# Entry of the second feed-forward block: statistics and normalising of tiles 4 to 7 placed behind the first half's modulation

## The chip, the core and the metric

The kernel runs on one core of a Trainium2 chip. Five engines work from queues of their own and meet only at semaphores: TensorE (PE, matrix products and transposes), VectorE (DVE), ScalarE (ACT), GpSimd (POOL) and SyncE (SP, which starts transfers). The metric is the device time of the whole program in microseconds (us), taken as the median of several runs. The rows shown here come from one profiled execution.

## What is computed

One layer of an encoder on 1024 positions of 1024 values, in fp32: a feed-forward block, a token mixer, and a second feed-forward block. The change touches only how the second feed-forward block begins.

```python
def _layer_norm(x):
    xf = x.astype(jnp.float32)
    mu = jnp.mean(xf, axis=-1, keepdims=True)
    var = jnp.mean(jnp.square(xf - mu), axis=-1, keepdims=True)
    return (xf - mu) * lax.rsqrt(var + LN_EPS)

def _swiglu(u, w_gate, w_up, w_down):
    return (jax.nn.silu(u @ w_gate) * (u @ w_up)) @ w_down

# in reference(), for each of the three sublayers
u = (_layer_norm(h) * (1.0 + scale) + shift).astype(h.dtype)
z = DEEPNORM_ALPHA * h.astype(jnp.float32) + resid_w * gate * fn(u)
return (_layer_norm(z) * ln_g[layer, j] + ln_b[layer, j]).astype(h.dtype)
...
h = sublayer(h, 2, lambda u: _swiglu(u, ffn2_w_gate[layer], ffn2_w_up[layer], ffn2_w_down[layer]), 0.5)
```

## The kernel before

The program is a row of phases with a barrier between them: the first feed-forward block (tag f1), the boundary into the mixer, two attention phases, the output projection, and the second feed-forward block (tag f2). Both blocks are `ffn_phase`. The rows give the tiles of both with one name (`f_...`); everything shown here lies in f2. The activations h are 8 tiles of 128 positions in `acc`; the tiles 0 to 3 are the first half (512 positions) and 4 to 7 the second.

**From h to the operands of the products.** For each tile VectorE takes the statistics (`ln.statistics`, lines 267 to 269: two bn_stats and an aggregate); ScalarE takes the root (`ln.root`, L278); VectorE works out the coefficients of a pair of tiles (`ln.coefficients`, L288 to L292); ScalarE writes the normalised tile (`ln.normalise`, called through `enter`, L297) into `f_nrm`. TensorE turns 128x128 blocks of it (`turn(y)`, L1272: four transposes, one 128x512 block in one of four PSUM banks). `turn(0)` to `turn(7)` are the first half, `turn(8)` to `turn(15)` the second; the first waits for 4 normalised tiles, the eighth for all 8. A turned block is modulated (scaled and shifted): the even y on VectorE (L1069), the odd ones on ScalarE (L887).

**fp32 in three products.** Each factor is split into a rounded high part, copied by ScalarE, and the low rest, subtracted by VectorE. `high0` and `low0` (L894, L1075) split the first half's blocks, `hi(o)` and `lo(o)` (L906, L1080) the weights of operand o, the lines 992, 994, 1153 and 1156 the second half's blocks. One product is 12 matmuls (4 steps of depth by high*high, high*low, low*high).

**The products at the entry.** `plain_product(p)`, p from 0 to 15, are the plain ones: p 0 to 7 work on the first half and p 8 to 15 on the second. Product p waits for its weights, `w_lo >= p % 8 + 1`. p 0 to 3 need the operands 0 to 3, p 4 to 7 the operands 4 to 7. The operands 0 to 3 are split among the first half's modulations. The operands 4 to 7 are split in the loop over k that treats the second half: in step k ScalarE and VectorE first modulate and split the second half's block k, and then operand 4 + k. The products after the plain ones (`product(j, i)`) also need sums of blocks that GpSimd takes from the modulated blocks (L843, L847, L850, L855).

**What sets the order.** It is written out by hand: each engine runs the instructions in the order of the code, and waits in front of one that isn't ready hold back all behind it. TensorE issues turns 0 to 7, products 0 and 1, turns 8 to 11, product 2, turns 12 to 15, product 3 and the rest. VectorE takes all 8 statistics, with the coefficients of tiles 0 to 3 among them, then the first half's modulation and splitting, and then the coefficients of tiles 4 to 7. ScalarE takes the roots of all tiles before the first half's copies, and normalises tiles 4 to 7 behind them. In f1 the tiles come normalised (`ready` is true, `ln` is None).

Of the kernel before, what the change touches and what calls it, by code (L numbers as in the profile page):

```python
# [18 lines left out]
KT = D // P  # L19
TT = S // P  # L20
# [607 lines left out]
def ffn_phase(nc, top, tag, mem, weights, j_mod, gate, resid, acc, mod_col, ident, hid, h_in, ada, lng, lnb, out,  # L628
# [67 lines left out]
    with ExitStack() as st:  # L696
        ps = Parts(nc, st).ps(tag + "_ps", [P, 8, NB])
        ln = None if ready else Normaliser(nc, top, mem.small, tag + "_in")
# [10 lines left out]
        def source(o):  # L709
            if o < RING:  # L710
                _, kk, j, f = plain(o)
                return raw[:, j, HK * kk:HK * kk + HK, P * f:P * f + P]
            j, i = seq[o - RING]
            r = raw[:, j % 2]
            if i == 1:
                return r[:, 0:HK, 0:P]
            if i == 2:
                return r[:, HK:KT, 0:P]
            if i == 4:
                return r[:, HK:KT, P:2 * P]  # L720
            return sums[:, (5, 6, 3, 7).index(i)]
# [7 lines left out]
        def half1(y):  # L729
            return (y - KT) // 2 + HK * (y % 2)  # L730
# [149 lines left out]
        def _(act):  # L880
# [88 lines left out]
            def enter(t):  # L969
                ln.normalise(act, nrm[t // 4][:, t % 4, :], acc[:, t, :], t)  # L970

            if ln is not None:
                for g in range(TT // 4):
                    ln.root(act, g)
                    enter(2 * g)
                    enter(2 * g + 1)
                for g in range(TT // 4, TT // 2):
                    ln.root(act, g)
            for y in range(HK):
                high0(y)  # L980
            for y in range(HK, KT):
                hi(y - HK)
                high0(y)
            if ln is not None:
                for t in range(TT // 2, TT):
                    enter(t)
            if keep is not None:
                act.wait_ge(kept, 16 * TT)
            for k in range(HK):
# [72 lines left out]
        def _(dve):  # L1062
# [62 lines left out]
            if ln is not None:  # L1125
                for t in range(TT // 2):
                    ln.statistics(dve, acc[:, t, :], t)
                    if t % 2:
                        ln.coefficients(dve, t // 2)
                for t in range(TT // 2, TT):  # L1130
                    ln.statistics(dve, acc[:, t, :], t)
            for y in range(KT):
                if y % 2 == 0:
                    modulate(y)
# [5 lines left out]
            lo(HK - 1)  # L1140
            low0(KT - 1)
            if ln is not None:
                ln.coefficients(dve, 2)
                ln.coefficients(dve, 3)
            if keep is not None:
                dve.wait_ge(kept, 16 * TT)
                dve.wait_ge(ln.normed, TT)
# [116 lines left out]
        def _(pe):  # L1264
            def turn(y):
                if ln is not None:
                    pe.wait_ge(ln.normed, TT // 2 * (y // KT + 1))
                if y >= 4:
                    pe.wait_ge(mod_done[y % 2], (y - 4) // 2 + 1)
                k = y if y < KT else half1(y)  # L1270
                for g in range(TT // 2):
                    done = nc.tensor.transpose(ps[:, TURN[y % 4], P * g:P * g + P],  # L1272
                                               nrm[y // KT][:, g, P * k:P * k + P], ident[:, :])
                done.then_inc(tr_done, 1)
# [10 lines left out]
            def plain_product(p):  # L1285

                half, kk, j, f = plain(p)
                o = p % 8
                pe.wait_ge(w_lo, o + 1)
                if half == 0:  # L1290
                    pe.wait_ge(lo0, HK * (kk + 1))
                    high, low = ((B11, B11), (B21, B21))[kk]
                else:
                    pe.wait_ge(mod_done[0], KT)
                    pe.wait_ge(mod_done[1], KT)
                    pe.wait_ge(lo_b if kk else lo_a, HK)
                    high, low = ((T4, T2), (B22, B22))[kk]
                multiply(PLAIN_BANK[half][j][f], o, uh[:, high], ul[:, low], kk == 0, kk == 1)
# [31 lines left out]
            def modulate(h):  # L1330
# [10 lines left out]
                                            start=h % 2 == 0, stop=h % 2 == 1, skip_group_check=True)  # L1341
                done.then_inc(a_mm, 1)

            for y in range(KT):
                turn(y)
            for p in range(PLAIN):
                plain_product(p)
                if p in (1, 2):
                    for y in range(4):
                        turn(KT + 4 * (p - 1) + y)  # L1350
            h = 0
            for n in range(PLAIN, N):
                product(*seq[n - PLAIN])
# [718 lines left out]
```

## Time and profile before

| | us |
|---|---|
| median of 3 runs | 2240.72 |
| lowest, highest | 2240.2, 2241.95 |
| span of the profiled execution | 2239.6 |

| engine | busy us, share of the span |
|---|---|
| TensorE, matmuls and transposes | 2040.5 (91%) |
| VectorE | 1100.8 (49%) |
| ScalarE | 753.1 (34%) |
| GpSimd | 462.5 (21%) |

In the profile L12 is line 12 of the kernel, and x4 is four instructions told in one row. A name of the form `f_ul<-acc,f_uh` is the tile written and the tiles read. "PEclk" is the clock that TensorE was granted, as a share of its full 2.4 GHz; only 1.00 and 0.50 (1.2 GHz) occur, and a number between them is a stretch that has some of each. The ends of matmuls are modelled, so starts are the better guide.

### The profile page before, as it was taken

What the parts mean: (1) busy time and instruction counts of PE and PEld (TensorE: products, weight loads), DVE (VectorE), ACT (ScalarE), POOL (GpSimd) and SP (SyncE); (2) the same over time, 40 slices, a digit from 0 to 9 for tenths busy, and PEclk for the clock granted to TensorE, in tenths of its full rate; (3) what the DMA queues carried; (4) which work ended last, traced back from release to release, by engine and by line L of the source; (5) the groups of instructions that cost most, each with busy time, mean ns of one, the idle gap of its engine ahead of it and who ended that gap; (6) DMA issues with size and microseconds to landing.
All of it is one profiled execution on the core that took longest, in us unless ns stands there. A gap on an engine that the chain in (4) does not pass through costs nothing. (4 is left out here: it accounts for less than half of the span.)

```text
span 2239.6 us, 27243 instructions
## 1 busy us (share of the span) xinstructions
PE 2040.5 (91%) x10350; PEld 1585.9 (71%) x10350; DVE 1100.8 (49%) x1891; ACT 753.1 (34%) x1253; POOL 462.5 (21%) x332
## 2 busy tenths in 40 slices
PE   3999999999999938999988889794999999999997
PEld 2777777777888826766666666673888888878885
DVE  4854544454346473344324443467743444443556
ACT  2533323333223243244323433315433333332331
POOL 0622222220004120000033202231622222100041
PEclk6999999999999969999999999897999999999998
DMA  6253444444644021100133021503222222265341
GB/s 254 82 160 124 157 156 130 155 142 168 246 147 167 30 104 47 57 28 29 56 82 60 19 49 38 197 38 120 76 89 74 90 80 90 90 237 195 141 168 49
DMA packets 157608, 247.34 MB, mean 110 GB/s; under 512 B 8097, under 2 KB 106673, under 8 KB 157361
## 3 DMA queue, kind: packets, MB, share of 16 engines
q1 hardware_dynamic: 126370, 211.36, 27.3%
q10 hardware_dynamic: 30096, 30.25, 4.4%
q0 software_dynamic: 1024, 4.13, 1.2%
q8 instruction: 77, 1.26, 0.2%
q14 instruction: 41, 0.34, 0.0%
HBM read 205.09 MB, written 40.63 MB: 110 GB/s over the span
## 5 line engine op out<-in xcount | busy, mean ns | idle before, releaser
L1280 PE MATMUL f_ps<-f_uh,f_ops 128*128 128x512 f32 x2496 | 794.1, 395 | 9.0 <-DVE acc L1119 4.9
L1280 PEld LDWEIGHTS f_ps<-f_uh,f_ops 128*128 128x128 f32 x2496 | 470.5, 188 | 137.8 <-issue 28.0
L1280 PE MATMUL f_ps<-f_ul,f_ops 128*128 128x512 f32 x1248 | 491.1, 394 | 0.0
L1380 PE MATMUL f_ps<-f_wdh,f_hdh 128*128 128x512 f32 x704 | 273.9, 389 | 0.0
L1380 PE MATMUL f_ps<-f_wdl,f_hdh 128*128 128x512 f32 x704 | 273.9, 389 | 0.0
L1380 PE MATMUL f_ps<-f_wdh,f_hdl 128*128 128x512 f32 x704 | 273.9, 389 | 0.0
L1280 PEld LDWEIGHTS f_ps<-f_ul,f_ops 128*128 128x128 f32 x1248 | 235.4, 189 | 48.2
L1180 DVE TENSOR_TENSOR f_wdl<-f_wd,f_wdh 128x2048 fp32r<-128x2048 f32 x44 | 107.3, 2438 | 227.2 <-ACT f_wdh L1010 227.2
L868 POOL TENSOR_TENSOR f_sums<-f_raw 128x512 f32<-128x512 f32 x80 | 107.4, 1343 | 444.4 <-DVE f_ops L1080 359.8
L1080 DVE TENSOR_TENSOR f_ops<-f_sums,f_ops 128x512 fp32r<-128x512 f32 x160 | 118.6, 741 | 153.9 <-ACT f_ops L906 153.9
L1010 ACT CAST f_wdh<-f_wd 128x2048 fp32r<-128x2048 f32 x44 | 83.9, 1907 | 302.5 <-PE f_ps L1380 259.5
L1754 PE MATMUL in_pj<-ut_hi,in_wh 128*128 128x512 f32 x376 | 151.1, 402 | 9.2 <-PEq L2036 4.8
L1080 DVE TENSOR_TENSOR f_ops<-f_raw,f_ops 128x512 fp32r<-128x512 f32 x136 | 99.0, 730 | 114.2 <-ACT f_ops L906 114.1
L1380 PEld LDWEIGHTS f_ps<-f_wdh,f_hdh 128*128 128x128 f32 x704 | 132.3, 188 | 27.7
L1380 PEld LDWEIGHTS f_ps<-f_wdl,f_hdh 128*128 128x128 f32 x704 | 132.2, 188 | 27.5
L1380 PEld LDWEIGHTS f_ps<-f_wdh,f_hdl 128*128 128x128 f32 x704 | 132.1, 188 | 27.3
L1754 PE MATMUL in_pj<-ut_lo,in_wh 128*128 128x512 f32 x376 | 148.2, 394 | 0.0
L1754 PE MATMUL in_pj<-ut_hi,in_wl 128*128 128x512 f32 x376 | 148.2, 394 | 0.0
L1119 DVE TENSOR_TENSOR acc<-acc,f_ps 128x512 f32<-128x512 f32 x120 | 82.5, 688 | 132.5 <-PE f_ps L1280 132.3
L875 POOL TENSOR_TENSOR acc<-acc,f_rows 128x1024 f32<-128x1024 f32 x12 | 36.1, 3006 | 384.5 <-ACT acc L297 384.5
L906 ACT CAST f_ops<-f_sums 128x512 fp32r<-128x512 f32 x160 | 95.6, 618 | 37.4 <-PE f_ps L1280 16.7
L906 ACT CAST f_ops<-f_raw 128x512 fp32r<-128x512 f32 x136 | 81.0, 620 | 31.8 <-PE f_ps L1280 21.0
(212 smaller groups left out, 2652.2 us busy)
## 6 DMA issues: line engine op xcount, KB each, us to landing
f_wd<-in_ffn_w_down SPq DMA_DIRECT2D x44, 1024.0 KB, 4.9
f_raw<-in_ffn_w_gate SPq DMA_DIRECT2D x22, 1024.0 KB, 5.5
f_raw<-in_ffn_w_up SPq DMA_DIRECT2D x22, 1024.0 KB, 5.4
f_hidden<-acc SPq DMA_DIRECT2D x88, 256.0 KB, 2.2
f_hd<-f_hidden SPq DMA_DIRECT2D x44, 512.0 KB, 5.6
f_aw<-in_w_ada ACTq DMA_DIRECT2D x28, 512.0 KB, 3.6
acc<-in_w_ada ACTq DMA_DIRECT2D x28, 512.0 KB, 3.5
in_raw<-in_w_in SPq DMA_DIRECT2D x24, 512.0 KB, 6.7
```

The costliest lines, as they stand in the source:

```text
L868: nc.gpsimd.tensor_tensor(sums[:, x], of, with_, how).then_inc(s_done, 1)
L875: nc.gpsimd.tensor_tensor(acc[:, t, :], acc[:, t, :], mem.rows[:, 0, :], ALU.mult).then_inc(gained, 1)
L906: nc.scalar.copy(op(o)[0], source(o)).then_inc(w_hi, 1)
L1010: nc.scalar.copy(mem.wdh[n % 3][:, :, :], mem.wd[:, n % 2]).then_inc(wd_hi, 1)
L1080: nc.vector.tensor_tensor(op(o)[1], source(o), op(o)[0].bitcast(F32), ALU.subtract).then_inc(w_lo, 1)
L1119: nc.vector.tensor_tensor(to, t_in, ps[:, bank, :], ALU.add).then_inc(done, 1)
L1180: nc.vector.tensor_tensor(mem.wdl[n % 3][:, :, :], mem.wd[:, n % 2], mem.wdh[n % 3][:, :, :].bitcast(F32), ALU.subtract).then_inc(wd_lo, 1)
L1280: done = nc.tensor.matmul(ps[:, bank, :], l[:, k, :], r[:, k, :], start=fresh and k == 0 and m == 0, stop=closed and k == HK - 1 and m == ...
L1380: done = nc.tensor.matmul(ps[:, b, :], l[n % 3][:, c, P * t:P * t + P], r[n % 3][:, c, NB * (b % 2):NB * (b % 2) + NB], start=p == 0 and c ...
L1754: last = nc.tensor.matmul(pj[:, half, :], l[:, k, j, :], r[:, k, NB * half:NB * half + NB], start=(k == 0 and n == 0), stop=(k == KT - 1 a ...
```

## The change

It moves instructions on three engines and adds or takes away none. On VectorE the statistics of tiles 4 to 7 go from ahead of the first half's modulation to behind it, in pairs with their coefficients. On ScalarE the roots of the tiles 4 to 7 go behind the first half's copies, each pair's roots ahead of its normalising. On TensorE, in f2 alone, turns 8 to 11 follow product 3 (they followed product 1) and turns 12 to 15 follow product 4 (they followed product 2). The transfers and GpSimd's instructions stay as they are.

```diff
@@ scalar engine
                     ln.root(act, g)
                     enter(2 * g)
                     enter(2 * g + 1)
-                for g in range(TT // 4, TT // 2):
-                    ln.root(act, g)
             for y in range(HK):
                 high0(y)
             for y in range(HK, KT):
                 hi(y - HK)
                 high0(y)
             if ln is not None:
-                for t in range(TT // 2, TT):
-                    enter(t)
+                for g in range(TT // 4, TT // 2):
+                    ln.root(act, g)
+                    enter(2 * g)
+                    enter(2 * g + 1)
@@ vector engine
                     if t % 2:
                         ln.coefficients(dve, t // 2)
-                for t in range(TT // 2, TT):
-                    ln.statistics(dve, acc[:, t, :], t)
             for y in range(KT):
...
             low0(KT - 1)
             if ln is not None:
-                ln.coefficients(dve, 2)
-                ln.coefficients(dve, 3)
+                for t in range(TT // 2, TT):
+                    ln.statistics(dve, acc[:, t, :], t)
+                    if t % 2:
+                        ln.coefficients(dve, t // 2)
@@ tensor engine
+            TURN_AFTER = (1, 2) if ready else (3, 4)
             for y in range(KT):
                 turn(y)
             for p in range(PLAIN):
                 plain_product(p)
-                if p in (1, 2):
+                if p in TURN_AFTER:
                     for y in range(4):
-                        turn(KT + 4 * (p - 1) + y)
+                        turn(KT + 4 * TURN_AFTER.index(p) + y)
```

On VectorE, where the first half's modulation begins and where the first half's splitting ends, before (`f_in_sm` holds the statistics, `f_b1m` the first half's modulated blocks, `f_ops_12698` the operands 0 to 3, `f_ops_12703` the operands 4 to 7):

```order
L268 BN_STATS f_in_sm<-acc 128x6
L269 BN_AGGR f_in_sm<-f_in_sm 128x2
L1069 TENSOR_SCALAR f_b1m<-f_ps,mod_col 128x512 x2
...
L1075 TENSOR_TENSOR f_ul<-f_b1m,f_uh 128x512
L288 RECIPROCAL f_in_sm<-f_in_sm 128x2
...
L292 SCALAR_TENSOR_TENSOR f_in_sm<-f_in_sm 128x2
L1069 TENSOR_SCALAR acc<-f_ps,mod_col 128x512 x2
L1153 TENSOR_TENSOR f_ul<-acc,f_uh 128x512
L1156 TENSOR_TENSOR f_ul<-acc,f_uh 128x512
L1080 TENSOR_TENSOR f_ops_12703<-f_raw,f_ops_12703 128x512
```

The same two places on VectorE in the changed kernel:

```order
L292 SCALAR_TENSOR_TENSOR f_in_sm<-f_in_sm 128x2
L1069 TENSOR_SCALAR f_b1m<-f_ps,mod_col 128x512 x2
...
L1075 TENSOR_TENSOR f_ul<-f_b1m,f_uh 128x512
L267 BN_STATS f_in_sm<-acc 128x6
L268 BN_STATS f_in_sm<-acc 128x6
L269 BN_AGGR f_in_sm<-f_in_sm 128x2
...
L292 SCALAR_TENSOR_TENSOR f_in_sm<-f_in_sm 128x2
L1069 TENSOR_SCALAR acc<-f_ps,mod_col 128x512 x2
L1153 TENSOR_TENSOR f_ul<-acc,f_uh 128x512
L1156 TENSOR_TENSOR f_ul<-acc,f_uh 128x512
L1080 TENSOR_TENSOR f_ops_12703<-f_raw,f_ops_12703 128x512
```

The modulation of the first half now follows the coefficients of tiles 2 and 3 directly, and the splitting of the first half is followed by four tiles' statistics and two sets of coefficients where only the two sets of coefficients stood.

On TensorE, around turns 8 to 15, before (`f_nrm_12705` holds the normalised tiles 4 to 7):

```order
L1280 MATMUL f_ps<-f_uh,f_ops_12698 128x512
L1272 MATMUL f_ps<-ident,f_nrm_12705 128x128 x16
L1280 MATMUL f_ps<-f_uh,f_ops_12698 128x512
...
L1280 MATMUL f_ps<-f_uh,f_ops_12698 128x512
L1272 MATMUL f_ps<-ident,f_nrm_12705 128x128 x16
L1280 MATMUL f_ps<-f_uh,f_ops_12698 128x512
```

And in the changed kernel:

```order
L1280 MATMUL f_ps<-f_uh,f_ops_12698 128x512
L1272 MATMUL f_ps<-ident,f_nrm_12705 128x128 x16
L1280 MATMUL f_ps<-f_uh,f_ops_12703 128x512
L1280 MATMUL f_ps<-f_ul,f_ops_12703 128x512
...
L1280 MATMUL f_ps<-f_uh,f_ops_12703 128x512
L1272 MATMUL f_ps<-ident,f_nrm_12705 128x128 x16
L1280 MATMUL f_ps<-f_uh,f_ops_12703 128x512
```

Both sets of turns stood in front of products that read the operands 0 to 3; both now stand in front of products that read the operands 4 to 7.

## Rows read from the trace of the kernel before

**Rows 1.** Chain of work that ended last: start us, us, what.

```profile
1548.44 4.64 ACT f_nrm L297 x4
1553.13 3.67 PE f_ps L1272 x16
1556.80 3.09 PE f_ps L1280 x12
1559.89 1.75 PE f_ps L1272 x16
1561.64 410.02 PE f_ps L1280 x1800
```

**Rows 2.** TensorE's waits from 1561 us to the end: us in total, times, longest.

```profile
PE f_ps L1280 <- DVE acc L1119: 2.5, 1, 2.5
```

**Rows 3.** Timeline of VectorE, entry of f2: start, us, instruction [idle before <- releaser].

```profile
1522.13 0.69 DVE L267 BATCH_NORM_STATS2 f_in_sm<-acc 128x6 f32<-128x512 f32 x1 [0.91 <-PEq L2044]
...
1530.82 0.69 DVE L267 BATCH_NORM_STATS2 f_in_sm<-acc 128x6 f32<-128x512 f32 x1
...
1536.44 1.48 DVE L1069 TENSOR_SCALAR f_b1m<-f_ps,mod_col 128x512 f32<-128x512 f32 x2
...
1547.46 0.16 DVE L288 RECIPROCAL f_in_sm<-f_in_sm 128x2 f32<-128x2 f32 x1
```

**Rows 4.** Timeline of ScalarE, same stretch.

```profile
1530.94 2.37 ACT L297 ACTIVATE f_nrm<-acc,f_in_sm 128x1024 f32<-128x1024 f32 x2 [1.03 <-DVE f_in_sm L292]
```

**Rows 5.** Timeline of TensorE, same stretch.

```profile
1533.37 3.67 PE L1272 MATMUL f_ps<-ident,f_nrm 128*128 128x128 f32 x16 [24.93 <-ACT f_nrm L297]
...
1542.48 0.50 PE L1280 MATMUL f_ps<-f_uh,f_ops 128*128 128x512 f32 x1 [1.33 <-DVE f_ops L1080]
...
1553.13 3.67 PE L1272 MATMUL f_ps<-ident,f_nrm 128*128 128x128 f32 x16 [4.87 <-ACT f_nrm L297]
```

**Rows 6.** Timeline of VectorE, second half's steps k = 0 to 3.

```profile
1554.39 0.81 DVE L1069 TENSOR_SCALAR acc<-f_ps,mod_col 128x512 f32<-128x512 f32 x1 [5.11 <-PE f_ps L1272]
...
1556.72 1.71 DVE L1153 TENSOR_TENSOR f_ul<-acc,f_uh 128x512 fp32r<-128x512 f32 x1
...
1558.95 0.68 DVE L1080 TENSOR_TENSOR f_ops<-f_raw,f_ops 128x512 fp32r<-128x512 f32 x1
1560.37 0.81 DVE L1069 TENSOR_SCALAR acc<-f_ps,mod_col 128x512 f32<-128x512 f32 x1 [0.74 <-PE f_ps L1272]
...
1564.20 0.68 DVE L1080 TENSOR_TENSOR f_ops<-f_raw,f_ops 128x512 fp32r<-128x512 f32 x1
...
1567.71 0.68 DVE L1153 TENSOR_TENSOR f_ul<-acc,f_uh 128x512 fp32r<-128x512 f32 x1
...
1569.51 2.48 DVE L1084 TENSOR_TENSOR f_ul<-acc,f_uh 128x512 fp32r<-128x512 f32 x4
```

**Rows 7.** Timeline of TensorE: turns 12 to 15 and product 3.

```profile
1559.73 1.91 PE L1272 MATMUL f_ps<-ident,f_nrm 128*128 128x128 f32 x16
1561.39 0.48 PE L1280 MATMUL f_ps<-f_uh,f_ops 128*128 128x512 f32 x1
```

**Rows 8.** By stretch: us, busy of PE, PEld, DVE, ACT, POOL, then PEclk, DMA share, GB/s.

```profile
1533.00:1537.00 4.00, 3.63 (x16) 3.28 (x16) 3.90 (x9) 1.23 (x5) 0.00 (x0) 0.51 1.02 416
1537.00:1540.00 3.00, 1.73 (x13) 1.28 (x12) 2.36 (x5) 2.77 (x6) 0.00 (x0) 1.00 0.94 384
...
1550.00:1553.00 3.00, 0.00 (x0) 0.00 (x0) 0.00 (x0) 3.00 (x3) 0.00 (x0) 0.59 0.00 0
...
1980.50:1984.00 3.50, 3.50 (x11) 2.72 (x10) 0.00 (x0) 0.00 (x0) 0.00 (x0) 0.52 0.23 80
```

**Rows 9.** Timeline of TensorE around its one late wait.

```profile
1979.60 0.47 PE L1280 MATMUL f_ps<-f_uh,f_ops 128*128 128x512 f32 x1 [2.46 <-DVE acc L1119]
...
1980.99 1.06 PE L1280 MATMUL f_ps<-f_uh,f_ops 128*128 128x512 f32 x2
...
1982.27 1.06 PE L1280 MATMUL f_ps<-f_uh,f_ops 128*128 128x512 f32 x2
```

## The prediction

> **What bounds the kernel now.** I read the page first (TensorE busy 91% of the span), then the chain of work that ended last, and then the timelines of each engine through the entry of the second block. The chain says where time at the entry counts [rows 1]. Up to 1553.13 it runs through ScalarE, which normalises tiles 4 to 7 (4.64 us). From 1553.13 it runs through TensorE: 16 transposes (turns 8 to 11), 12 matmuls (product 2), 16 transposes (turns 12 to 15), and then 1800 matmuls in 410.02 us with nothing between them. From 1561 us to the end TensorE waits for another engine once, for 2.5 us [rows 2]. So TensorE is the bound from turn 8 on, and whatever reaches it later than now there is paid in full at the end; no slack follows that could give it back. I therefore compare the time at which product 8 (the first on the second half) can start. Now, product 3 starts behind the last turns at about 1561.6 and five products (3 to 7) follow. A product is 12 matmuls at 410.02 / 1800 = 0.228 us, that is 2.73 us, so product 8 starts at 1561.64 + 5 x 2.73 = **1575.3**.
>
> **Step 1, the first half starts earlier.** Turn 0 begins at 1533.37, as soon as tiles 0 to 3 are normalised (1530.94 + 2.37) [rows 4, 5], but VectorE modulates the first block only at 1536.44, behind the statistics of tiles 4 to 7, which began at 1530.82 [rows 3]. With these moved away it begins when the turn is ready. In the second half, turn 8 begins at 1553.13 and VectorE's modulation at 1554.39, 1.26 later [rows 5, 6]; so here 1533.37 + 1.26 = 1534.63, which is 1.81 us earlier. ScalarE's copies and modulations wait for VectorE's first one and pace the rest, so the whole first half moves by 1.8: product 0 from 1542.48 [rows 5] to 1540.7, the end of splitting on VectorE from 1547.46 [rows 3] to 1545.65. ScalarE's four roots, which move too, are hidden in the same way.
>
> **Step 2, the second half's normalising is late.** Behind 1545.65 VectorE now has four statistics and two sets of coefficients, between them roots and normalising on ScalarE: the very sequence that tiles 0 to 3 went through from 1522.13 [rows 3] to the start of turn 0 at 1533.37 [rows 5], 11.24 us. Turn 8 thus starts at 1545.65 + 11.24 = **1556.9**, against 1553.13 now: 3.8 us later. Ahead of it lie four products and not two: 1540.7 + 4 x 2.73 = 1551.6. TensorE waits 5.3 us, about what it waits now (4.87, [rows 5]). That alone would not be a loss, since two products (5.46 us) have been done in those 3.8 us: 1.7 us would be won.
>
> **Step 3, what stands behind the turns.** Now product 2 follows turn 11, and its weights are long split. In the changed kernel product 4 follows, and operand 4 is split by VectorE only behind the second half's modulations. Now it is ready at 1558.95 + 0.68 = 1559.63, 6.50 us behind the start of turn 8 [rows 5, 6]. Nothing in these 6.5 us depends on what TensorE runs behind the turns, so product 4 starts at 1556.9 + 6.5 = **1563.4**. The turns take 3.67 us at the low clock, as now [rows 5], to 1560.6; 2.8 us of new waiting. This is the wait that takes the old one's place.
>
> **Step 4, the clock.** TensorE's granted clock fell to 0.50 between 1550 and 1553, with TensorE idle since 1548.3 [rows 5], and was still low when the turns ran (3.67 us for 16, against 1.75 for turns 12 to 15) [rows 1, 8]. A wait of 5.3 us should do the same. Then come 3.67 us of transposes, 2.8 us of nothing and product 4. That a wait of this size is enough by itself shows late in the program: one of 2.46 us was followed by a stretch at 0.52 [rows 8, 9]; three matmuls start 1982.27 - 1980.99 = 1.28 us apart there, 0.427 each. So I take product 4 at 1.2 GHz: 12 x 0.427 = 5.1 us, to 1568.5. At 2.4 GHz it would take 2.73, to 1566.1; these are the two ends. I take the slow one, since the clock is low ahead of the turns and a wait lies on either side of them.
>
> Before turn 0, TensorE had run nothing for 24.93 us, and 16 transposes alone brought the clock from 0.51 to 1.00 [rows 5, 8]. The Trainium skill ("TensorE: Matmul & The Clock Gate", "Part 4: PE-mode transpose") says that the high clock doesn't engage for transposes, because they don't count as TensorE being busy; by that product 4 would be slow without exception, and the sum would be the one I take. The trace disagrees with that rule.
>
> **Step 5, the second set of turns.** Turns 12 to 15 now stand behind product 4, and VectorE's step k = 1 begins with the modulation of turn 12's block, ahead of operand 5. Now that modulation starts 0.64 us behind turn 12 at 2.4 GHz (1559.73 to 1560.37, [rows 6, 7]), or 1.26 at 1.2 GHz (step 1). Operand 5 is ready at 1564.20 + 0.68, 4.51 behind the modulation [rows 6], but two subtractions of this stretch are slow, running beside GpSimd; free of it, three take 1.8 together (1567.71 to 1569.51), and with the modulation's 0.8 that is 2.6 us. GpSimd has had its work for k = 1 in the meantime, so I take the short one, with the low clock: 1.26 + 2.6 = 3.9 us, between 3.2 (0.64 + 2.6) and 5.1 (0.64 + 4.51). Product 5 starts at 1568.5 + 3.9 = **1572.4**. TensorE's turns take 1.7 to 3.7 of it, so up to 2.2 us are waiting.
>
> **Step 6, products 5 to 7.** Operand 6 takes VectorE one such step more, 2.6 to some 3.4 with GpSimd beside it, say 3.0 us, against 2.73 for a product: 0.3 us. Operand 7 has no modulation on VectorE and is in time. Product 8 starts at 1572.4 + 3 x 2.73 + 0.3 = **1580.9**.
>
> **The sum.** 1580.9 - 1575.3 = 5.6 us later. By parts: the earlier first half -1.8, the later statistics +5.6 (together +3.8 at turn 8: 11.24 from the end of splitting to turn 8, where 5.67 pass now), two products already done -5.5, the wait for operand 4 +2.8, the clock +2.4, the second set of turns with the wait for operand 5 +2.2 over the 1.7 they cost now, and 0.3 for operand 6; product 2 at the low clock, which now costs 3.09 [rows 1] and not 2.73, is gone, -0.4. That is 5.5, and 5.6 before rounding. Nothing later is in danger of adding: the sums on GpSimd and the block splits move by the same 4 to 6 us and the products that need them move too. The second half's tile loads, stores and the copy of h to memory are not moved. The span would be 2239.6 + 5.6 = 2245.2; the median of the runs is 1.1 above the profiled span, so the forecast is 2240.7 + 5.6 = **2246.3**.
>
> **The rivals.** *A, forecast*: as above, +4.5 to +6.7. *B, the clock comes back*: the transposes of turns 8 to 11 raise it, as the first 16 did, and the wait behind them doesn't take it away. Product 4 saves 2.4 and turn 12 some 0.6: +2.6, up to +4.4 where the clock is high for a part; 2243.3. For it: the rise after transposes alone [rows 8]. Against: 2.46 us of waiting were enough for a fall [rows 9]. *C, all is hidden*: the other side. It takes the statistics, roots and normalising to be covered by products 0 to 3 and operand 4 to be split when the turns end. Then product 8 would start at 1540.7 + 8 x 2.73 + 2 x 1.75 = 1566.0, that is 9.3 us sooner: 2231.4. It decides at 5.9 us from the end of splitting (1545.65) to turn 8 (1551.6), where the same sequence now takes 11.24, and operand 4 has to be split within 1.75 us and not 6.5. If only operand 4 were in time, 1.7 us would be won: 2239.0. Against both stand rows 3 and 6, which are measured durations of these very instructions. *D, a second fall*: the waits before products 5 and 6 let the clock fall once more; such a stretch, 3.5 us at half clock [rows 8], costs 1.7, and slow subtractions beside GpSimd 1.2: +6.7 to +8.5, 2248.0.
>
> **How the numbers follow.** A 0.58, D 0.15, B 0.22, C with its half 0.03, and 0.02 for what I don't see, on either side. For this kernel 0.2% is 4.5 us, about what a measurement can tell from no change, and A's low end lies on it: a twelfth of A goes to "same". Slower: 0.53 + 0.15 + 0.01 = 0.69; same: 0.05 + 0.22 + 0.01 = 0.28; faster 0.03. The range goes from B, with 0.3 us for the medians, to the middle of D with 1 us more: 2243.0 to 2249.0. It leaves out C, the edges of B and D and the unseen, some 0.13.
>
> **What would show it.** In the changed kernel's timeline: VectorE's first L1069 some 1.8 us earlier behind turn 0; four products in a row, then a TensorE wait of about 5.3 us on ScalarE's L297; 16 transposes; a second wait of 2 to 3 us on VectorE's L1080; product 4 at the low clock, starts 0.427 apart; a wait on L1080 behind turns 12 to 15; and no wait of TensorE afterwards but the known one at the end of the gate and up products. Step 2 is wrong if turn 8 starts earlier than 1555, step 3 if no wait follows turn 11, step 4 if product 4 takes under 3 us. The forecast falls if TensorE starts product 8 before 1578.

## The result

| | us |
|---|---|
| changed kernel, median of 9 runs | 2245.16 (2242.47 to 2247.57) |
| kernel before, median of 9 runs | 2240.2 (2237.35 to 2241.95) |
| ratio | 1.0022, 95% interval 1.0013 to 1.0032 |
| span of the profiled execution | 2243.1 |

The change made the kernel slower by 5.0 us, 0.22%. The forecast was 5.6 us slower, 2246.3.

The first half's entry in the changed kernel. These are the timelines of TensorE and VectorE (start us, us, instruction, idle time before it and what ended it); they answer to [rows 5] and [rows 3]:

```profile
1532.61 4.84 PE L1272 MATMUL f_ps<-ident,f_nrm 128*128 128x128 f32 x28 [24.91 <-ACT f_nrm L297]
...
1540.06 0.50 PE L1280 MATMUL f_ps<-f_uh,f_ops 128*128 128x512 f32 x1 [1.53 <-DVE f_ops L1080]
```

```profile
1521.39 0.69 DVE L267 BATCH_NORM_STATS2 f_in_sm<-acc 128x6 f32<-128x512 f32 x1
...
1533.76 0.81 DVE L1069 TENSOR_SCALAR f_b1m<-f_ps,mod_col 128x512 f32<-128x512 f32 x1 [3.61 <-PE f_ps L1272]
...
1544.86 0.68 DVE L267 BATCH_NORM_STATS2 f_in_sm<-acc 128x6 f32<-128x512 f32 x1
```

Everything in this execution lies 0.76 us earlier than in the profile of before (turn 0 at 1532.61 against 1533.37), so I count from turn 0. VectorE's first modulation is 1.15 us behind it (before 3.07), product 0 7.45 (before 9.11), the end of the first half's splitting 12.25 (before 14.09).

The second half's entry, TensorE in the changed kernel, answering to [rows 5, 7]:

```profile
1556.08 3.47 PE L1272 MATMUL f_ps<-ident,f_nrm 128*128 128x128 f32 x16 [4.75 <-ACT f_nrm L297]
1562.39 0.50 PE L1280 MATMUL f_ps<-f_uh,f_ops 128*128 128x512 f32 x1 [2.85 <-DVE f_ops L1080]
...
1564.09 1.05 PE L1280 MATMUL f_ps<-f_uh,f_ops 128*128 128x512 f32 x2
...
1565.37 1.05 PE L1280 MATMUL f_ps<-f_uh,f_ops 128*128 128x512 f32 x2
...
1566.85 1.91 PE L1272 MATMUL f_ps<-ident,f_nrm 128*128 128x128 f32 x16
1570.15 0.50 PE L1280 MATMUL f_ps<-f_uh,f_ops 128*128 128x512 f32 x1 [1.39 <-DVE f_ops L1080]
```

Turn 8 starts 23.47 us behind turn 0, where it was 19.76; the wait ahead of it is as long as it was. Behind the turns stand two waits that the kernel before doesn't have, 2.85 us for operand 4 and 1.39 us for operand 5, both ended by VectorE's L1080. Between them product 4 takes 1566.85 - 1562.39 = 4.46 us, with most of its matmuls 0.427 us apart (1564.09 to 1565.37 is three of them).

The granted clock in the same stretch (last columns PEclk, DMA share, GB/s), answering to [rows 8]:

```profile
1553.00:1556.00 3.00, 0.00 (x0) 0.00 (x0) 0.51 (x4) 2.35 (x2) 0.00 (x0) 1.00 0.00 0
1556.00:1559.50 3.50, 3.42 (x16) 3.07 (x16) 1.58 (x3) 1.58 (x4) 1.41 (x2) 0.55 0.02 5
1560.00:1562.00 2.00, 0.00 (x0) 0.00 (x0) 2.00 (x3) 2.00 (x5) 0.77 (x2) 1.00 0.00 0
1563.50:1566.50 3.00, 3.00 (x8) 2.33 (x8) 0.00 (x0) 0.00 (x0) 2.46 (x2) 0.50 0.00 0
1567.00:1570.00 3.00, 1.76 (x17) 1.52 (x14) 2.51 (x4) 2.08 (x4) 0.42 (x1) 1.00 0.00 0
```

The clock fell twice: for turns 8 to 11, and again inside product 4. Between them, behind the turns, it was at 2.4 GHz.

The chain of work that ended last, answering to [rows 1], and TensorE's waits from 1545 us on, answering to [rows 2]:

```profile
1570.15 405.04 PE f_ps L1280 x1776
```

```profile
PE f_ps L1272 <- ACT f_nrm L297: 4.7, 1, 4.7
PE f_ps L1280 <- DVE f_ops L1080: 4.2, 2, 2.9
PE f_ps L1280 <- DVE acc L1119: 2.5, 1, 2.5
```

Behind product 5 nothing gives anything back. The unbroken stretch of matmuls ends 1570.15 + 405.04 - 1532.61 = 442.58 us behind turn 0; before, 1561.64 + 410.02 - 1533.37 = 438.29. That is 4.3 us later at the same piece of work, against 5.0 by the medians. I call this number, turn 0 to the end of the stretch, E in what follows. It comes from one profiled execution of each kernel, so it also holds whatever the clock did in that one.

### The profile page after: what moved, and what is told of

The parts are those of the page before. It is cut to its first block and busy times, and to the rows that moved or that the text cites. A ratio compares the mean times of both kernels' runs of the same rounds, so it can differ in the third digit from the quotient of the medians.

```text
span 2243.1 us, 27243 instructions
## 1 busy us (share of the span) xinstructions
PE 2042.8 (91%) x10350; PEld 1587.7 (71%) x10350; DVE 1098.1 (49%) x1891; ACT 753.5 (34%) x1253; POOL 463.1 (21%) x332
## 3 DMA queue, kind: packets, MB, share of 16 engines
q8 instruction: 77, 1.26, 0.2%
## 5 line engine op out<-in xcount | busy, mean ns | idle before, releaser
L1080 DVE TENSOR_TENSOR f_ops<-f_sums,f_ops 128x512 fp32r<-128x512 f32 x160 | 118.1, 738 | 152.2 <-ACT f_ops L906 152.2
L1080 DVE TENSOR_TENSOR f_ops<-f_raw,f_ops 128x512 fp32r<-128x512 f32 x136 | 99.2, 731 | 113.7 <-ACT f_ops L906 113.6
L906 ACT CAST f_ops<-f_raw 128x512 fp32r<-128x512 f32 x136 | 81.0, 620 | 31.3 <-PE f_ps L1280 20.6
```

The costliest lines, as they stand in the source:

```text
L906: nc.scalar.copy(op(o)[0], source(o)).then_inc(w_hi, 1)
L1080: nc.vector.tensor_tensor(op(o)[1], source(o), op(o)[0].bitcast(F32), ALU.subtract).then_inc(w_lo, 1)
```

## The experiments

The theory was that of the prediction: turn 8 is late since the statistics stand behind the first half, and the turns' new place in front of products 4 and 5 turns that into new waits and a low clock. The rival was that one of the two moves is the whole loss. Each ratio is to the kernel before on the same chip. Not run was the kernel before with only the operands split early; no wait of its TensorE from turn 8 on is for an operand of the entry [rows 1, 2], so little could be won there.

| kernel | ratio, 95% interval | E minus that of before, us |
|---|---|---|
| changed kernel | 1.0022, 1.0013 to 1.0032 | +4.3 |
| changed, turns behind 1 and 2 | 1.0013, 1.0004 to 1.0022 | +3.3 |
| before, turns behind 3 and 4 | 1.0002, 0.9993 to 1.0011 | +2.8 |
| changed, operands 4 to 7 early | 0.9996, 0.9987 to 1.0005 | -0.7 |
| changed, wait filled | 1.0015, 1.0006 to 1.0024 | +3.9 |
| before, wait filled | 0.9991, 0.9982 to 1.0 | -1.4 |
| statistics in two pairs, turns behind 4 and 5 | 0.9996, 0.9987 to 1.0005 | -1.2 |
| the same, turns behind 3 and 4 | 0.9981, 0.9972 to 0.999 | -3.5 |
| before, operands early, turns behind 3 and 4 | 0.9985, 0.9976 to 0.9994 | -3.3 |
| that one, T4 split together | 0.9977, 0.9968 to 0.9986 | -5.9 |
| two pairs, turns behind 3 and 4, T4 together | 0.997, 0.9958 to 0.9982 | -7.3 |

### The turns put back

```diff
-            TURN_AFTER = (1, 2) if ready else (3, 4)
+            TURN_AFTER = (1, 2)
```

> The changed kernel, with the turns of the second half back behind products 1 and 2, so only the statistics, coefficients and roots are moved. Theory (new waits on operands 4 and 5 behind the turns are what is lost): turn 8 comes 23.5 us behind turn 0, as in the changed kernel, TensorE waits about 10 us ahead of it, and behind it nothing waits, so product 8 comes 3.7 us later than before: 2243.9, faster than the changed kernel by about 1. Rival (the turn positions are not to blame, four products ahead of the wait are worth their 5.5 us): 2243.9 is then too good and the kernel loses 5 us or more against the changed one, 2250.

Measured: 2242.78 us, ratio 1.0013. The chain of work in this kernel:

```profile
1555.46 3.62 PE f_ps L1272 x16
1559.08 2.75 PE f_ps L1280 x12
1561.84 1.75 PE f_ps L1272 x16
1563.58 410.01 PE f_ps L1280 x1800
```

Turn 8 is 23.46 us behind turn 0 (1532.00), the same as in the changed kernel. The wait ahead of it has grown to 10.24 us, and nothing waits behind it. The loss is 3.0 us by the medians and 3.3 by E, near the 3.7 of the theory and far from the rival's 2250. So the late statistics cost 3 us by themselves, and with four products ahead of the wait the kernel does no better: the 5.5 us of products done early are all given back and about 1 to 2 us more. The ratios' intervals overlap, so the size of that last part rests on the traces.

### The turns moved alone

```diff
-                if p in (1, 2):
+                if p in TURN_AFTER:    # (1, 2) in f1, (3, 4) in f2
```

> The kernel before, with only the turns moved behind products 3 and 4; statistics and normalising as before. Theory: products 0 to 3 run without a wait and turn 8 starts about 20.2 us behind turn 0 at the high clock; product 4 then waits for operand 4, some 5 us behind the start of turn 8 (3 us of wait), product 5 for operand 5 as in the changed kernel. Product 8 comes 2.4 us sooner than before, 2237.8, or 2239.5 if the clock falls in the wait ahead of product 4. Rival (the late turns themselves cost the time, whatever stands ahead of them): slower than before, 2242 or more.

Measured: 2240.58 us, ratio 1.0002, runs from 2235.52 to 2246.63. The medians decide little: the ratio's interval holds no change, the theory's 2239.5 for a clock that falls (the clock did fall) and, at its very end, the rival's 2242; only the 2237.8 without a fall is missed. TensorE:

```profile
1557.49 1.91 PE L1272 MATMUL f_ps<-ident,f_nrm 128*128 128x128 f32 x16
1563.35 0.79 PE L1280 MATMUL f_ps<-f_uh,f_ops 128*128 128x512 f32 x1 [3.95 <-DVE f_ops L1080]
1568.61 1.91 PE L1272 MATMUL f_ps<-ident,f_nrm 128*128 128x128 f32 x16
1571.92 0.50 PE L1280 MATMUL f_ps<-f_uh,f_ops 128*128 128x512 f32 x1 [1.40 <-DVE f_ops L1080]
```

The two waits on L1080 are there without any late statistics, so they belong to the turns' place. Turn 8 had no wait ahead of it, as expected, but operand 4 was ready 1563.35 - 1557.49 = 5.86 us behind it and not 5. Quick turns help VectorE's step little (the reason shows two experiments on). Product 4 ran wholly at the low clock (5.42 us in the chain of work). In this execution the clock, low since before turn 0, also rose only during the first products (12.75 us for the 48 matmuls of products 0 to 3, against 4 x 2.73 = 10.9); that is 1.8 us of the +2.8 at which E stands, where the medians have 0.8. It was also the slowest of the 11 executions.

### The operands 4 to 7 split early

```diff
+                for o in range(HK, KT):      # ScalarE, ahead of the roots of tiles 4 to 7
+                    hi(o)
...
+                for o in range(HK, KT):      # VectorE, behind the coefficients of tiles 6 and 7
+                    lo(o)
```

In the loop over k, `hi(HK + k)` and `lo(HK + k)` then stand for f1 alone.

> The changed kernel, with the operands 4 to 7 split while tiles 4 to 7 are normalised, ahead of the second half's steps. This takes away what products 4 and 5 wait for. Theory: turn 8 stays at 23.5 us behind turn 0, product 4 follows turn 11 and product 5 turn 15 without a wait and TensorE's clock is back soon behind the turns: 2.9 + 1.4 us of waits and most of the 1.7 us of low clock in product 4 are won back, 6 us against the changed kernel; 2238.9 to 2239.9, level with before or better by 1. Rival (turn 8 being late is the whole loss, and the waits behind it only follow): within 1.5 us of the changed kernel, 2244 to 2245.

Measured: 2238.21 us, ratio 0.9996, a little under the 2238.9 to 2239.9 of the theory; the rival (2244 or more) is out. Its interval (0.9987 to 1.0005) lies clear of the changed kernel's (1.0013 to 1.0032). The chain of work:

```profile
1555.62 3.63 PE f_ps L1278 x16
1559.24 2.75 PE f_ps L1286 x12
1561.99 1.75 PE f_ps L1278 x16
1563.74 19.18 PE f_ps L1286 x84
```

Turn 8 is as late as ever (23.49 us behind turn 0, 1532.13), but product 4 follows the turns at once and at 2.4 GHz (2.75 us for 12 matmuls), and product 5 as well. E falls by 5.0 us against the changed kernel. This settles the cause: without what products 4 and 5 wait for, the whole loss is gone, though turn 8 is as late as before; against the kernel before, the late turn 8 is paid for by the two products done ahead of it. That is the gain of 1.7 us that step 2 of the prediction had without these waits; by E 0.7 remain, because a new wait appears later, ahead of product 19 (`product(2, 6)`):

```profile
1603.16 0.47 PE L1286 MATMUL f_ps<-f_uh,f_ops 128*128 128x512 f32 x1 [1.14 <-ACT acc L925]
```

### TensorE's wait filled

To price the clock, 18 matmuls whose results are not used go into the wait ahead of turn 8, once in the changed kernel and once in the kernel before.

```diff
+                if p == 3 and not ready:      # p == 1 in the kernel before
+                    pe.wait_ge(mod_done[0], 3)
+                    for n in range(18):
+                        nc.tensor.matmul(ps[:, TURN[0], :], op(0)[0][:, 0, :], uh[:, B11, 0, :], start=True, stop=True,
+                                         skip_group_check=True)
```

> The changed kernel, with 18 matmuls whose results are not used (4.1 us at the high clock) in the wait ahead of turn 8; they add work only where TensorE would wait. It prices the clock. Theory: turn 8 is not moved, the turns 8 to 11 run at 2.4 GHz and end 1.7 us sooner, so operand 4 is ready 5.0 to 5.5 us behind turn 8 in place of 6.3, and product 4 takes 2.7 to 3.5 us and not 4.5: 2.0 to 3.0 us faster than the changed kernel, 2242.2 to 2243.2. Rival (the clock plays no part, only the splitting sets the pace): within 0.5 us of the changed kernel, 2245.2.

Measured: 2242.73 us, ratio 1.0015, in the range expected; but its interval and the changed kernel's overlap, and by E only 0.4 us are won, which is the rival's side. The trace shows why. TensorE, then VectorE and GpSimd:

```profile
1556.06 1.97 PE L1272 MATMUL f_ps<-ident,f_nrm 128*128 128x128 f32 x16 [0.64 <-ACT f_nrm L297]
1561.97 0.65 PE L1280 MATMUL f_ps<-f_uh,f_ops 128*128 128x512 f32 x1 [3.95 <-DVE f_ops L1080]
```

```profile
1558.57 1.07 DVE L1153 TENSOR_TENSOR f_ul<-acc,f_uh 128x512 fp32r<-128x512 f32 x1
1559.56 1.75 DVE L1156 TENSOR_TENSOR f_ul<-acc,f_uh 128x512 fp32r<-128x512 f32 x1
1561.24 0.68 DVE L1080 TENSOR_TENSOR f_ops<-f_raw,f_ops 128x512 fp32r<-128x512 f32 x1
```

```profile
1559.04 1.72 POOL L847 TENSOR_TENSOR acc<-acc 128x512 f32<-128x512 f32 x1
```

The same two subtractions in the changed kernel:

```profile
1559.46 1.68 DVE L1153 TENSOR_TENSOR f_ul<-acc,f_uh 128x512 fp32r<-128x512 f32 x1
1561.06 0.68 DVE L1156 TENSOR_TENSOR f_ul<-acc,f_uh 128x512 fp32r<-128x512 f32 x1
```

The turns take 1.97 us and not 3.47, yet operand 4 is ready 5.91 us behind turn 8 and not 5.0 to 5.5. VectorE begins the two subtractions 0.9 us sooner behind turn 8 (2.51 us, where it was 3.38), but beside GpSimd's sum they take 1.07 and 1.75 us, where they took 1.68 and 0.68: half of the 0.9 is lost again. The time won in the turns goes into a longer wait (3.95), and product 4 is slow again (4.61 us in the chain). Here the clock is a consequence of the waits more than a cause of the loss. And since product 4 kept its low clock, no run prices that part by itself; 4.46 us against 2.73 is read off the traces.

> The kernel before with 18 matmuls whose results are not used (4.1 us at the high clock) in TensorE's wait of 4.87 us ahead of turn 8. Nothing else is moved, and no product waits behind the turns, so it prices the low clock at the entry: turns 8 to 11 in 1.8 us and not 3.7, product 2 in 2.73 and not 3.09: 2.2 us sooner, 2237.5. Rival (the clock falls at another place for it, or the turns do not bind): within 0.7 us of the kernel before.

Measured: 2238.63 us, ratio 0.9991 (0.9982 to 1.0). The chain of work, L1351 being the 18 matmuls:

```profile
1542.02 7.37 PE f_ps L1280 x24
1549.39 4.12 PE f_ps L1351 x18
1553.51 1.75 PE f_ps L1272 x16
1555.25 2.75 PE f_ps L1280 x12
```

Where nothing waits behind the turns, the clock's price is direct: turns 1.75 against 3.67 us, product 2 2.75 against 3.09, 2.3 together. E wins 1.4 of it. In this execution products 0 and 1 had a stretch of low clock of their own (7.37 us for 24 matmuls, 5.5 at the high clock), which pushed the 18 matmuls past the end of the wait, so turn 8 started 0.8 us later behind turn 0 than before (1553.51 - 1532.90 = 20.6). The median is 1.4 us lower than that of before, the ratio says 2.0, and its interval reaches up to no change.

### The same order with the causes removed

In the kernel before, with statistics and roots where they were: the operands 4 to 7 are split behind the normalising of tiles 4 to 7, and the turns stand behind products 3 and 4.

> The kernel before with its statistics, coefficients and roots where they were, the operands 4 to 7 split directly behind the normalising of tiles 4 to 7, and the turns behind products 3 and 4. It keeps the changed kernel's order on TensorE and takes away both what made turn 8 late and what products 4 and 5 waited for. Theory: turn 8 follows product 3 without a wait, 20.0 us behind turn 0, at the high clock, nothing waits behind it; TensorE alone would give 6 us sooner than before (2234.2), the chain through GpSimd some 4 (2236). Rival (the turns' place behind products 3 and 4 costs time in itself): 2239.7 or slower, as with the turns moved alone.

Measured: 2235.93 us, ratio 0.9985, as expected from the chain through GpSimd. Turn 8 starts 20.2 us behind turn 0, and TensorE runs from product 0 to product 18 without a wait. So the turns' place, which cost time in the changed kernel, costs nothing where the operands are ready. The late statistics do still cost something then: with them, and the same operands and turns, E was -0.7 and here it is -3.3, from one execution each (the ratios' intervals overlap). But TensorE alone would have given 6 us; a wait of 3.2 us stands behind product 18:

```profile
1596.87 0.68 DVE L1087 TENSOR_TENSOR f_ul<-acc,f_uh 128x512 fp32r<-128x512 f32 x1
...
1597.58 0.59 ACT L925 COPY acc<-f_ps 128x512 f32<-128x512 f32 x1 [7.51 <-DVE f_ul L1087]
...
1598.31 0.47 PE L1286 MATMUL f_ps<-f_uh,f_ops 128*128 128x512 f32 x1 [3.18 <-ACT acc L925]
```

ScalarE stood 7.51 us in front of a copy that may only overwrite its block when the last sum of blocks (T4) is split (L1087), and TensorE waited for that copy.

### The statistics in two pairs

On the changed kernel: tiles 4 and 5 get their statistics ahead of the first modulation, where VectorE waited 3.61 us for turn 0; tiles 6 and 7 behind the first half; operands early as above, on ScalarE operands 4 to 6 ahead of the normalising of tiles 4 and 5 and operand 7 ahead of that of tiles 6 and 7. VectorE's part:

```diff
+                ln.statistics(dve, acc[:, 4, :], 4)      # ahead of the first half's modulation
+                ln.statistics(dve, acc[:, 5, :], 5)
...
-                for t in range(TT // 2, TT):
-                    ln.statistics(dve, acc[:, t, :], t)
-                    if t % 2:
-                        ln.coefficients(dve, t // 2)
+                ln.coefficients(dve, 2)
+                ln.statistics(dve, acc[:, 6, :], 6)
+                ln.statistics(dve, acc[:, 7, :], 7)
+                lo(4)
+                ln.coefficients(dve, 3)
+                for o in (5, 6, 7):
+                    lo(o)
```

> Built from the changed kernel: the statistics of tiles 4 and 5 stand ahead of the first modulation (VectorE waits there for turn 0 anyway), those of 6 and 7 behind the first half, the operands 4 to 7 are split while tiles 4 to 7 are normalised, and the turns 8 to 11 follow product 4, 12 to 15 product 5. Turn 8 should start some 21 us behind turn 0 with TensorE working until then and the clock high. If only TensorE bounds what follows, product 8 starts 8.5 us sooner than in the kernel before: 2231.5. Rival (the sums of blocks on GpSimd and their splitting, which start behind turn 8, bind as soon as TensorE is early; with the operands split early alone, the product that waited for them stood 47.5 us behind turn 8, against 52.2 before): 4 us sooner, 2235.8.

> As the one with the turns behind products 4 and 5, but behind 3 and 4: turn 8 starts when tiles 4 to 7 are normalised, some 20 us behind turn 0, with about 1.5 us of wait ahead of it. If TensorE bounds the rest, 1 to 1.5 us slower than with products 4 and 5: 2233. If the chain through GpSimd from turn 8 on bounds it, about 1 us faster than that one, 2235.0.

Measured: 2239.04 us (0.9996) with the turns behind products 4 and 5, and 2235.8 us (0.9981) behind 3 and 4. The second is as the chain through GpSimd gives it, the first is 3 us slower than even its rival had it (2235.8). In the second, turn 8 comes 20.0 us behind turn 0 with 1.28 us of wait. In the first TensorE works through to turn 8, 21.3 us behind turn 0, and pays later. Its waits from 1545 us on, and the clock behind the first of them:

```profile
PE f_ps L1292 <- ACT acc L925: 3.1, 1, 3.1
PE f_ps L1292 <- DVE acc L1125: 2.5, 1, 2.5
PE f_ps L1292 <- DVE f_ul L1164: 1.2, 1, 1.2
```

```profile
1600.00:1604.00 4.00, 1.77 (x4) 1.50 (x5) 4.00 (x6) 2.11 (x4) 1.97 (x2) 0.67 0.35 131
1604.00:1608.00 4.00, 4.00 (x11) 3.09 (x10) 1.64 (x3) 1.41 (x3) 0.00 (x0) 0.50 0.75 240
```

In the second kernel the wait for L925 is 1.9 us and PEclk from 1604 to 1608 us is 0.75. Counted from turn 0, turn 8 comes 1.3 us later in the first kernel and product 19, which waits for L925, 1.2 us later (67.85 against 66.66 us); the 1608 matmuls from there on take 369.26 us against 368.11. So keeping TensorE busy by a product put in front of turn 8 delays all that hangs on turn 8, and once that chain binds, the delay comes back, in these executions with a longer stretch of low clock behind it. The two give 2.3 us of the medians' 3.2; the rest is not explained.

### T4 split together

T2 and T4 are two of the sums of blocks. The four blocks of T4 are now split directly behind those of T2, in two kernels: the one with the causes removed, and the one with two pairs and the turns behind products 3 and 4. On VectorE:

```diff
                     for k in range(HK):
                         sum_lo(T2, k)
+                    if ln is not None:
+                        for k in range(HK):
+                            sum_lo(T4, k)
-                if RING + 4 < n <= PLAIN:
+                if ln is None and RING + 4 < n <= PLAIN:
                     sum_lo(T4, n - RING - 5)
```

and likewise `sum_hi` on ScalarE.

> The kernel before with the operands 4 to 7 early and the turns behind products 3 and 4, and besides that the four blocks of the last sum (T4) split together directly behind those of T2, and not one by one between the weights' sums. In that kernel TensorE waited 3.2 us about 68 us behind turn 0 for a ScalarE copy that itself waits until T4 is split. If this order is what took back the gain of TensorE being early: the wait goes, 3 us sooner than without it, 2232.8. Rival (GpSimd's rate binds, and the products then wait for the weights' sums in place of T4): within 1 us of it, 2235.9.

> The same order of T4 on top of the kernel with the statistics split in two pairs and the turns behind products 3 and 4. Its late wait was 1.9 us, with a stretch of low clock behind it. First reason (order of T4): 1.9 us of wait and most of the 1.7 us of low clock go, 2232.5. Rival (GpSimd's rate): 2235.8.

Measured: 2234.66 us (0.9977) and 2231.76 us (0.997). TensorE's waits from 1545 us on, of the first and of the second kernel:

```profile
PE f_ps L1293 <- DVE acc L1126: 2.5, 1, 2.5
PE f_ps L1293 <- ACT acc L935: 0.2, 1, 0.2
```

```profile
PE f_ps L1299 <- DVE acc L1129: 2.5, 1, 2.5
PE f_ps L1291 <- ACT f_nrm L297: 1.3, 1, 1.3
```

The waits of 3.2 and 1.9 us are gone but for 0.2, and E falls by 2.6 and 3.7 us. So it was the order in which VectorE and ScalarE took T4, not GpSimd's rate, that bound it; the rival is out by the traces. By the ratios alone neither step is clear: the intervals overlap in both pairs. The last kernel (median of 6 runs) is the best of all, 0.3% faster than before and 0.5% faster than the changed one.

## Why the prediction was right, point by point

| step | forecast, us | in the changed kernel's trace |
|---|---|---|
| 1, first half earlier | 1.8 | 1.84 (end of splitting), 1.66 (product 0) |
| 2, turn 8 later | 3.8 | 3.71 |
| 2, wait ahead of turn 8 | 5.3 | 4.75 |
| 3, start of turn 8 to product 4 | 6.5 | 6.31 |
| 3, wait behind turn 11 | 2.8 | 2.85 |
| 4, product 4 | 5.1 | 4.46 |
| 5, turn 12 to product 5 | 3.9 | 3.30 |
| 6, product 5 to product 8 | 8.5 | 8.5 |
| all, at the end of the stretch | 5.6 | 4.3; by the medians 5.0 |

The two misses, in steps 4 and 5, are 1.2 us together and account for the 5.6 being 4.3 in the trace; that the medians have 5.0, nearer to the forecast, is not the sum's doing. The prediction adds its listed parts up to 5.5; they are 5.6, as its own sum by times has it.

**Steps 1 to 3** held to within 0.2 us, but for the wait ahead of turn 8: product 0 moved by 1.66 and not 1.8, and the profile counts product 3 as busy up to its last matmul's modelled end. Durations of the same instructions, taken from the neighbouring stretch in which the same engines run the same sequence, were enough.

**Step 4** had the right sign and was 0.6 us too large. I took the clock to be low from turn 8 through product 4. It came back behind the turns and fell again, so product 4 began at 2.4 GHz and ended at it. The forecast took the slow end; the truth lay at three quarters of the way between the two ends of 2.7 and 5.1. Rival B, a clock that comes back and stays, came true by half: it came back, as B had it, and then fell, as B had not. B's own edge was +4.4 for a clock that is high for a part of product 4, and A's low end +4.5; the trace's +4.3 lies at that edge, the medians' +5.0 in A. So the forecast's mechanism of waits held, and its clock in product 4 only for the larger part. With the Trainium skill's rule that the high clock doesn't engage for transposes ("TensorE: Matmul & The Clock Gate", "Part 4: PE-mode transpose") the trace of the changed kernel disagrees again, as [rows 8] did: TensorE ran nothing but transposes between 1556.08 and the wait, and the clock rose from 0.55 to 1.00.

**Step 5** was 0.6 us too large, again by the clock: the turns 12 to 15 ran at 2.4 GHz (VectorE's modulation 0.64 us behind turn 12), so the short end of 3.2 held. That the subtractions would run free of GpSimd was right.

**Step 6** held: product 8 starts at some 1578.7, 8.5 us behind product 5. That is 46.1 us behind turn 0, where the prediction had 47.5.

**Rival C** (all hidden) was far off, as rows 3 and 6 said. **Rival D** (a second fall before product 5 or 6) did not show.

What the prediction did not see is that operand 4's readiness hardly depends on the clock: it used 6.5 us for slow turns, and my estimates for quick turns in two experiments (5, and 5.0 to 5.5) were short by 0.4 to 0.9.

## What to carry to other kernels

When work that an engine waits for is moved behind other work, look at what stands behind the moved wait in each queue, not only ahead of it: here the late statistics were paid for by two products done early, and the whole loss was gone once the operands were no longer split behind the second half's modulation, of which they needed nothing. An instruction that could run in an idle stretch but stands behind a wait that isn't its own is the first thing to move. When the bounding engine is freed, another chain can bind later, here at product 19; find its gate in the trace (here a copy that waited 7.5 us for an unrelated split) before adding more.

## What the hardware showed beyond the forecast

**The same wait does not always cost the same.** The late wait of 2.46 us [rows 9] is in every kernel here. Behind it 12 matmuls took 4.58 us in the chain of work of before and 4.52 in the changed kernel's; with the clock at 1.00 throughout, as in the kernel before with the wait filled, they took 3.00. The row of before and that one:

```profile
1979.60 4.58 PE f_ps L1280 x12
```

```profile
1977.71 3.00 PE f_ps L1280 x12
```

So in 9 of the 12 profiled executions the clock fell behind this wait, and in 3 it did not. That is 1.6 us of spread from one wait, and runs of one kernel spread by 5 to 11 us here. A gain of 2 us is hard to see in medians of 11 runs, whose ratio has an interval of 2 us to either side. A trace counted from a common event shows which wait came and went, but one execution also carries its own falls of the clock: 1.8 us of E with the turns moved alone, 0.8 in the kernel before with the wait filled.

**VectorE and GpSimd beside each other.** A 128x512 subtraction on VectorE takes 0.68 us alone and 1.7 us beside GpSimd's sums. Which one is slowed changed when TensorE's turns ended 1.5 us sooner: L1153 (1.68 us) in the changed kernel, L1156 (1.75 us) with the wait filled, and then GpSimd's L847 too took 1.72 us, where it took 1.26. Half of what the quicker turns gave VectorE went there.
